# Turning H by VectorE and small DMA copies instead of TensorE, in a two-layer encoder kernel

## What is computed

```python
def swiglu(x, w_gate, w_up, w_down):      # D_MODEL = 1024, D_FF = 2816
    return (jax.nn.silu(x @ w_gate) * (x @ w_up)) @ w_down

h = swiglu(x, ffn_w_gate[l, 0], ffn_w_up[l, 0], ffn_w_down[l, 0])
x = layer_norm(DN_ALPHA * x + 0.5 * h, ln_g[l, 0], ln_b[l, 0])
...
h = swiglu(x, ffn_w_gate[l, 1], ffn_w_up[l, 1], ffn_w_down[l, 1])
x = layer_norm(DN_ALPHA * x + 0.5 * h, ln_g[l, 3], ln_b[l, 3])
```

## Time and profile before

| | us |
|---|---|
| median of 3 runs | 1258.87 (1258.11 to 1260.05) |
| profiled execution, whole | 1258.38 |
| its span in the profile | 1256.3 |
| PE busy | 1236.3 |
| DVE busy | 775.5 |
| ACT busy | 598.4 |
| POOL busy | 156.4 |
| DMA queue of SP, share of the 16 engines | 50.6% |

### The profile page before, as it was taken

One profiled execution on the slowest core, in us unless ns is written; L12 is line 12 of the kernel. 1 busy time (PEld: TensorE's weight loads), 2 busy tenths in 40 slices (PEclk: granted clock), 3 DMA queues, 4 the chain that ended last, 5 costly groups with the idle time before them and its releaser, 6 DMA issues.

```text
span 1256.3 us, 16132 instructions
## 1 busy us (share of the span) xinstructions
PE 1236.3 (98%) x6696; PEld 1060.3 (84%) x6696; DVE 775.5 (62%) x1017; ACT 598.4 (48%) x731; POOL 156.4 (12%) x161
## 2 busy tenths in 40 slices
PE   7999999999999999999999999999999999999997
PEld 6888888898899888888888888889987998888886
DVE  5667746687564665545466676665877747655454
ACT  5444554557443554343445345545556444534432
POOL 1026800000101000000000067300001100000000
PEclk9999999999999999999999999999999999999999
DMA  9755555532456375655565565546334535655550
GB/s 334 264 170 190 177 175 163 174 127 75 150 190 204 107 252 179 200 176 193 199 203 188 181 196 174 196 153 185 102 102 134 185 118 168 213 189 190 179 200 34
DMA packets 160232, 219.44 MB, mean 175 GB/s; under 512 B 6912, under 2 KB 136064, under 8 KB 160160
## 3 DMA queue, kind: packets, MB, share of 16 engines
q1 hardware_dynamic: 156864, 206.60, 50.6%
q0 software_dynamic: 3152, 11.76, 2.9%
q10 hardware_dynamic: 144, 0.07, 0.0%
HBM read 217.34 MB, written 1.05 MB: 174 GB/s over the span
## 4 chain that ended last, share of the span: by engine, by line
PE 96%; SPq 1%; DMA 1%; issue 1%; ACT 1%; DVE 1%; DVEq 0%; POOLq 0%; POOL 0%
PE PS L518 28%; PE PS L520 28%; PE PS L519 28%; PE PS L549 2%; PE PS L1138 1%; PE PS L1162 1%; PE PS L601 1%; PE PS L928 1%; DMA RAW<-in_ffn_w_down 1%; SPq L407 1%; PE PS L828 1%; PE PS L840 1%; PE PS L861 1%; PE PS L905 1%; PE PS L778 0%
## 5 line engine op out<-in xcount | busy, mean ns | idle before, releaser
L1645 DVE TENSOR_TENSOR WL<-RAW,WH 128x2048 fp32r<-128x2048 f32 (+1 forms) x199 | 448.5, 2259 | 243.7 <-ACT WH L1219 243.3
L1219 ACT ACTIVATE WH<-RAW 128x2048 fp32r<-128x2048 f32 (+1 forms) x199 | 370.7, 1872 | 157.7 <-DMA RAW<-in_ffn_w_up 122.6
L518 PE MATMUL PS<-WH,XH 128*128 128x512 f32 x762 | 304.5, 400 | 1.6 <-DVE WL L1645 1.2
L520 PE MATMUL PS<-WH,XL 128*128 128x512 f32 x762 | 297.8, 391 | 0.0
L519 PE MATMUL PS<-WL,XH 128*128 128x512 f32 x762 | 297.7, 391 | 0.0
L518 PEld LDWEIGHTS PS<-WH,XH 128*128 128x128 f32 x762 | 143.5, 188 | 32.0 <-DVE WL L1645 2.0
L520 PEld LDWEIGHTS PS<-WH,XL 128*128 128x128 f32 x762 | 143.3, 188 | 30.5
L519 PEld LDWEIGHTS PS<-WL,XH 128*128 128x128 f32 x762 | 143.7, 189 | 28.3 <-issue 0.5
L518 PE MATMUL PS<-WH,HH 128*128 128x512 f32 x352 | 137.7, 391 | 0.1
L520 PE MATMUL PS<-WH,HL 128*128 128x512 f32 x352 | 137.1, 389 | 0.0
L519 PE MATMUL PS<-WL,HH 128*128 128x512 f32 x352 | 137.0, 389 | 0.0
(11 more groups left out here) (351 smaller groups left out, 1783.5 us busy)
## 6 DMA issues: line engine op xcount, KB each, us to landing
RAW<-in_ffn_w_down SPq DMA_DIRECT2D x88, 512.0 KB, 4.4
RAW<-in_ffn_w_gate SPq DMA_DIRECT2D x87, 512.0 KB, 3.9
RAW<-in_ffn_w_up SPq DMA_DIRECT2D x87, 512.0 KB, 5.0
RAW<-in_w_in SPq DMA_DIRECT2D x44, 512.0 KB, 4.5
RAW<-in_xattn_wkv SPq DMA_DIRECT2D x32, 512.0 KB, 4.3
RAW<-in_xattn_wq SPq DMA_DIRECT2D x16, 512.0 KB, 4.1
RAW<-in_w_out SPq DMA_DIRECT2D x12, 512.0 KB, 4.4
RAW<-in_xattn_wo SPq DMA_DIRECT2D x12, 512.0 KB, 4.1
```

Of the source, the lines that this page charges most:

```text
L518: nc.tensor.matmul(out_ap, sh, mh, start=first, stop=False)
L520: return nc.tensor.matmul(out_ap, sl, mh, start=False, stop=last)
L1219: return nc.scalar.activation(dst, src, ACT.Copy)
L1645: return v.tensor_tensor(dst, full, hi.bitcast(F32), ALU.subtract)
```

## The change

The change leaves the last block of each part as it was and turns H of the other ten blocks in another way. `h_mul` writes HB in a layout with the column half first. DVE then turns every 32x32 square of H within its own 32-partition group, with one transpose instruction over 128 partitions (HB to HB4, which lies over SG). SP issues sixteen DMA copies of 32 partitions x 512 bytes, one for each pair of source and destination partition group, from HB4 to HT4 (which lies over HB). ACT's `h_hi` and DVE's `low` read HT4 instead of PSUM. `turn_h` on PE is called for the last block only. In SP's order the copies of block j-1 stand after the first gate-up load and before the second gate-up load of block j+1 (for block 0: before its down load; for block 9: at the end). ACT now waits in `h_hi` for the copies and for the down product of the block before; DVE waits for its own HL before the next `h_mul`.

```diff
-        HB = sb("HB", [P, TT, FB], F32, f8_at)
+        HB = sb("HB", [P, 2, TT, P], F32, f8_at)
         SG = sb("SG", [P, TT, FB], F32, f8_at + 2048)
+        HB4 = sb("HB4", [P, 4, 4, 32], F32, f8_at + 2048)
+        HT4 = sb("HT4", [P, 4, 4, 32], F32, f8_at)
...
+            def move_h(l, s, blk):
+
+                sp.wait_ge(hB_turned.sem, hB_turned.at(l, 10 * s + blk + 1))
+                for i in range(4):
+                    for j in range(4):
+                        sp.dma_start(HT4[32 * j:32 * j + 32, i], HB4[32 * i:32 * i + 32, j]).then_inc(hT_moved.sem, 16)
+
...
                 for j in range(BLOCKS - 1):
                     load_gu(l, s, 2 + 3 * j, j + 1, 0)
+                    if j > 1:
+                        move_h(l, s, j - 1)
                     load_gu(l, s, 3 + 3 * j, j + 1, 1)
+                    if j == 1:
+                        move_h(l, s, 0)
                     load_down(l, s, 4 + 3 * j, j)
...
                 load_down(l, s, FFN_UNITS - 1, BLOCKS - 1)
+                move_h(l, s, BLOCKS - 2)
...
-                                                 HB[:, t, fc * P:fc * P + P], ident)
+                                                 HB[:, fc, t, :], ident)
...
-                turn_h(l, s, 0)
...
-                    turn_h(l, s, j)
...
-                turn_h(l, s, j)
...
             def h_hi(l, s, blk, dst=HH):
-                act.wait_ge(hT_psum.sem, hT_psum.at(l, 11 * s + blk + 1))
-                copy(dst[:, :, :], PS[:, 6, :].rearrange("p (c n) -> p c n", c=2)).then_inc(hT_hi.sem, 1)
+                if blk == BLOCKS - 1:
+                    act.wait_ge(hT_psum.sem, hT_psum.at(l, s + 1))
+                    copy(dst[:, :, :], PS[:, 6, :].rearrange("p (c n) -> p c n", c=2)).then_inc(hT_hi.sem, 1)
+                    return
+                act.wait_ge(hT_moved.sem, hT_moved.at(l, 256 * (10 * s + blk + 1)))
+                if blk > 0:
+                    act.wait_ge(unit_used.sem, UNIT[l, f"F{s}", 3 * blk + 1] + 1)
+                copy(dst[:, :, :].rearrange("p f (t i n) -> p (f t) i n", t=TT, i=4),
+                     HT4[:, :, :, :].rearrange("p i c n -> p c i n")).then_inc(hT_hi.sem, 1)
...
             def h_mul(l, base, t):
                 dve.wait_ge(sg_done.sem, sg_done.at(l, base + t))
-                v.tensor_tensor(HB[:, t, :], SG[:, t, :], PS[:, 4 + t, FB:2 * FB], ALU.mult).then_inc(h_ready.sem, 1)
+                v.tensor_tensor(HB[:, :, t, :], SG[:, t, :].rearrange("p (f n) -> p f n", f=2),
+                                PS[:, 4 + t, FB:2 * FB].rearrange("p (f n) -> p f n", f=2), ALU.mult).then_inc(h_ready.sem, 1)
+
+            def turn_h(l, s, blk):
+
+                dve.wait_ge(h_ready.sem, h_ready.at(l, 22 * s + 2 * blk + 2))
+                v.transpose(HB4[:, :, :, :].rearrange("p j c n -> p c j n"),
+                            HB[:, :, :, :].rearrange("p f t (j n) -> p (f t) j n", j=4)).then_inc(hB_turned.sem, 1)
...
                 def step(j, last):
                     dve.wait_ge(hT_hi.sem, hT_hi.at(l, j + (11 * s + 1)))
-                    low(HL[:, :, :], PS[:, 6, :].rearrange("p (c n) -> p c n", c=2), HH[:, :, :])\
-                        .then_inc(hT_lo.sem, 1)
-                    split()
+                    low(HL[:, :, :].rearrange("p f (t i n) -> p (f t) i n", t=TT, i=4),
+                        HT4[:, :, :, :].rearrange("p i c n -> p c i n"),
+                        HH[:, :, :].rearrange("p f (t i n) -> p (f t) i n", t=TT, i=4)).then_inc(hT_lo.sem, 1)
+                    split()
+                    dve.wait_ge(hT_lo.sem, hT_lo.at(l, 11 * s + j + 1))
                     h_mul(l, j * 2 + (22 * s + 3), 0)
                     h_mul(l, j * 2 + (22 * s + 3), 1)
+                    if not last:
+                        turn_h(l, s, j + 1)
```

More of the change, by code:

```diff
@@ L276, in build @@
         h_ready = Event("h_ready", 2 * BLOCKS * TT)
-        hT_psum = Event("hT_psum", 2 * BLOCKS)
+        hB_turned = Event("hB_turned", 2 * (BLOCKS - 1))
+        hT_moved = Event("hT_moved", 2 * (BLOCKS - 1) * 256)
+        hT_psum = Event("hT_psum", 2)
         hT_hi = Event("hT_hi", 2 * BLOCKS)
@@ L1800, in ffn @@
                     h_mul(l, 22 * s + 1, 1)
+                    turn_h(l, s, 0)
                     split()
```

## The result

The changed kernel takes 1444.66 us (median of 4, 1442.98 to 1448.32) against 1258.49 us for the kernel before (median of 4): 1.148 times as long, 95% interval 1.146 to 1.150, 186 us more. The forecast was slower, 1300 us, with 1250 to 1340: the direction and the path are there, but the loss is 4.5 times the 41.7 us of the sum.

A forecast was written before the change was run, and what follows sets the result against it. The prediction took PE as the bound before and a 17.93 us ring through SP's queue after. Its four parts added 41.7 us, the 17.9 us gain inside, to 1258.4, giving 1300 us, range 1250 to 1340.

The forecast's parts named there:

- the sum: Over four feed-forward parts, extra time of 13.5, 9.5, 9.5 and 9.2 us: 41.7 us slower in total, 17.9 gain included.
- The turns on PE: Four transposes per turn take 0.447 us of PE; 40 of 44 turns go, taking 17.9 us off PE.
- The path: On SP the copies stand before load 3b+6, which ACT and DVE split before the next h_mul and turn.
- the ring: Turn, copies, load, ACT split, DVE split, h_mul, next turn: 17.93 us a block, against 16.32 that PE needs.
- PE waiting for HL: Sign of a wrong path: if in every block, the copies' landing and not the load behind them is the bound.
- DVE's turn: The new 32x32 turn on DVE: 0.65 us, plus 0.15 for wait and signal; bounds 0.41 and 1.23.
- The landing: A copy lands 2.0 to 2.1 us after its issue on SP, the shortest shown.
- The issue: One copy's issue on SP costs 0.425 us, the middle of 0.375 and 0.48; sixteen take 6.8 us.
- the slope that the prediction gives: Each 0.1 us in the cost of one issue on SP is 64 us of kernel time (16 x 0.1 x 40).
- A: Rival: copies issued on SP at 0.32 us or less, PE stays the bound, 1240.5 us; chance 0.13.
- B: Rival: same mechanism, with DVE's turn at twice its cost or issues at 0.48, 1324 to 1335 us; inside the main 0.82.
- C: Rival: copies held on SP as issues are at the kernel's start, 1.4 us each, some 1920 us; chance 0.02.

## Why the prediction was right and wrong
**The turns on PE, 17.9 us.** Right: the kernel without copies is 18.6 us under the kernel before as measured beside it (1258.35). Starts of matmuls, not their durations, gave it.

**The path.** Right. The copies' place in SP's queue closes a ring that PE isn't in; each of its six steps stands in the trace, in the order named, and twelve, eight and no copies follow the ring. What the prediction named as the sign of a wrong path, PE waiting for HL, is there in 24 blocks; it doesn't mean what the prediction says, since the load behind the copies, and not their landing, is what ACT and so the ring wait for last.

**DVE's turn, 0.65 us.** It takes 0.71. The estimate of 1.24 us worked out from the Trainium skill ("VectorE: DVE Perf Modes", The three transpose paths) is too high for this shape and type; the rows of two-input operations were the better guide.

**The landing, 2.0 to 2.1 us.** It takes 1.8 in the median, and it isn't in the ring.

**The issue, 0.425 us. This step failed.** It was taken as the middle of 0.375 and 0.48, and that was called the range, because "all issues shown have a floor that doesn't shrink with bytes". All issues shown had one end in HBM; the copies had none, and cost 0.63 from start to start, 0.64 on average with the long ones. No row could show that, and the bound was drawn from the rows as if they were of the same kind. Even for that kind it was narrow. The second load of a gate-up unit in the kernel before (start, us, line):
```profile
1103.05 0.51 SPq L407 DMA_DIRECT2D RAW<-in_ffn_w_up  x1
```
That is 0.55 from start to start, and 1380 us by the slope that the prediction gives, 64 us for each 0.1 us. With 0.64 the slope gives 1438, 7 below what was measured. The rounds say the same: a round is 3.65 us longer than the 17.93 of the sum, 3.47 of it by the copies, and the sum has 35 such rounds, which is 128 of the 145 us that were missed. The first round of each part took 17.4 to 18.4 us where the sum has 14.8, which is 12 more in the four parts together. With issues of 0.477 from HBM the kernel was at 1340, and the sum gives 1333, low by the same 7 us.

The Trainium skill's rule that initiating a DMA is usually small relative to the DMA itself ("DMA: Bandwidth & Descriptors", Issuing engines are not separate DMA queues) holds for the gate and up loads of 512 KB here (0.37 and 0.51 us of SP, 3.9 and 5.0 to landing in the median), and less so for these copies: 0.59 us of SP for 16 KB that land 1.8 us after the issue. The 50 ns of dispatch that the prediction took from its anatomy table stand there for DMAs that GpSimd issues, and no issue on SP here was shorter than 0.3 us.

**Rivals.** A (cheap issues) would have been right in its consequence: with no copies the whole gain is there, at 1240. Its condition is off by a factor of two. B had the mechanism and too small a price. C gave over 1 us an issue for a reason (much in flight); one issue in each of nine rounds took that long, and why was not looked into.

**PE's clock** was not in the sum. Behind the wait of 3.8 us above, the matmuls ran at nearly half clock. In the changed kernel PE isn't in the ring, so I put no part of the 186 us on it, but no run filled PE's waits there. Where the ring goes through PE, filling the waits gave back 41 us. How much it adds in the first blocks of the parts, where PE waited for HH for 4.96 us and the first matmuls behind it took 0.63 to 0.77 us, was not separated. PE's rows of the changed kernel (start, us, line):
```profile
527.31 0.77 PE L534 MATMUL PS<-WH,HH 128*128 128x512 f32 x1 [4.96 <-ACT HH L1232]
527.87 0.63 PE L535 MATMUL PS<-WL,HH 128*128 128x512 f32 x1
528.30 0.63 PE L536 MATMUL PS<-WH,HL 128*128 128x512 f32 x1
```

## What to carry to other kernels
Before work is moved off the bound engine, follow what stands behind it in every queue it is moved to, and look for a ring that leads back to it; its length against the bound's own period decides, and the bend is sharp: no copies 1240 us, eight 1250, twelve 1347, sixteen 1445. A DMA's price is paid twice, in transfer and in the queue that issues it. For the small copies here the second was the larger, 10 us of the queue for sixteen of them against 1.8 to the landing of one: count issues first, then bytes. Where the trace has no operation of the new kind, bounds from its neighbours are bounds only for that kind; name the respect in which the new one differs (here: where both ends lie) and leave room for it.

## What the runs showed of the hardware
- A DMA issue on SP with both ends in SBUF holds the queue 0.59 us in a row and 0.51 as the first of a row, against 0.42 and 0.33 for the same copies with their source in HBM. Between 16 and 128 rows and 4 and 64 KB the medians differ by 0.03 us at most. On POOL's queue the copies with both ends in SBUF take 0.49 us each, and 3.1 to landing in the median.
- A turn of 128x512 float32 in 32x32 squares takes DVE 0.71 us, as long as a two-input operation of that shape.
- Right behind a wait of PE of 3.8 us the granted TensorE clock was 0.53 over 7 us, nearly all at its lower level of 1.2 GHz; with matmuls that compute nothing in these waits it was 1.00 there and 0.998 over the span, and the kernel was 41 us shorter.
